# Dilated attention: three PSUM banks for the turns and three for the scores, where it was two and four

## What is computed

```python
proj = (x @ w_in).reshape(B, T, 3, ATT_GROUPS, ATT_HEADS, ATT_HEAD_DIM)   # q, k, v; 3 groups; 16 heads of 64
for g, (window, dil) in enumerate(((128, 1), (512, 4), (2048, 16))):
    s = q @ k.T * hd ** -0.5 + bias[g], masked to a band with step dil
    p_g = softmax(s);  o_g = p_g @ v;  lse_g = log of the denominator
w = softmax over the three groups of lse
return (sum_g w_g * o_g) @ w_out
```

## Time and profile before

| what | us |
|---|---|
| median of 3 runs | 2949.99 |
| lowest and highest | 2945.5, 2952.11 |
| profiled execution, its own time | 2954.55 |
| its span, first to last instruction | 2952.8 |
| PE busy | 2788.1 (94%) |
| DVE busy | 1300.7 (44%) |
| ACT busy | 1017.7 (34%) |
| POOL busy | 191.2 (6%) |

### The profile page before, as it was taken

One profiled execution on the slowest core, in us unless ns is written; L12 is line 12 of the kernel. 1 busy time (PEld: TensorE's weight loads), 2 busy tenths in 40 slices (PEclk: granted clock), 3 DMA queues, 4 the chain that ended last, 5 costly groups with the idle time before them and its releaser, 6 DMA issues.

```text
span 2952.8 us, 40584 instructions
## 1 busy us (share of the span) xinstructions
PE 2788.1 (94%) x17764; PEld 2437.8 (83%) x17764; DVE 1300.7 (44%) x1663; ACT 1017.7 (34%) x1270; POOL 191.2 (6%) x182
## 2 busy tenths in 40 slices
PE   6999999799999999999998979999999989988998
PEld 4778878678787777877887768999989989977997
DVE  3333233264532324333335465556555554554544
ACT  3222232231321223322224244443634444453443
POOL 1000010010100001000001000001010010043100
PEclk9999999967999999999998989999999999999999
DMA  6434354400434335334333214555444545753452
GB/s 241 153 116 164 118 167 136 150 24 1 143 129 137 135 127 173 124 119 157 123 120 133 72 35 152 193 169 172 131 155 161 184 145 191 213 132 108 129 195 77
DMA packets 398176, 406.13 MB, mean 138 GB/s; under 512 B 7216, under 2 KB 397056, under 8 KB 397872
## 3 DMA queue, kind: packets, MB, share of 16 engines
q1 hardware_dynamic: 398000, 403.54, 41.6%
HBM read 402.38 MB, written 1.12 MB: 137 GB/s over the span
## 4 chain that ended last, share of the span: by engine, by line
PE 89%; DVE 5%; ACT 3%; DMA 1%; issue 1%; POOL 0%; SPq 0%; POOLq 0%; ACTq 0%; DVEq 0%
PE bank L96 89%; DVE w_lo L107 1%; ACT w_hi L103 1%; PE bank L99 1%; ACT df_e L104 1%; POOL acc L107 0%; DVE tmp L115 0%; ACT x_hi L103 0%; DMA w_raw<-in_ada_w 0%; SPq L133 0%; DVE x_lo L115 0%; DVE df_e L115 0%; DMA w_raw<-in_even_w_in 0%; DMA w_raw<-in_mix_w_out 0%; DVE df_sc L124 0%
## 5 line engine op out<-in xcount | busy, mean ns | idle before, releaser
L107 DVE TENSOR_TENSOR w_lo<-w_raw,w_hi 128x2048 fp32r<-128x2048 f32 (+2 forms) x331 | 693.8, 2099 | 951.2 <-ACT w_hi L103 950.5
L96 PE MATMUL bank<-x_hi,w_hi 128*128 128x256 f32 (+1 forms) x3128 | 1042.5, 333 | 41.7 <-DVE x_lo L115 25.8
L96 PE MATMUL bank<-x_lo,w_hi 128*128 128x256 f32 (+1 forms) x3128 | 1031.6, 330 | 0.0
L96 PE MATMUL bank<-x_hi,w_lo 128*128 128x256 f32 (+1 forms) x3128 | 1030.9, 330 | 0.0
L103 ACT ACTIVATE w_hi<-w_raw 128x2048 fp32r<-128x2048 f32 (+2 forms) x331 | 578.6, 1751 | 626.1 <-PE bank L96 256.4
L96 PEld LDWEIGHTS bank<-x_hi,w_hi 128*128 128x128 f32 x3128 | 604.7, 193 | 109.9 <-issue 59.8
L96 PEld LDWEIGHTS bank<-x_hi,w_lo 128*128 128x128 f32 x3128 | 604.2, 193 | 51.3
L96 PEld LDWEIGHTS bank<-x_lo,w_hi 128*128 128x128 f32 x3128 | 604.9, 193 | 50.5 <-issue 0.7
L96 PE MATMUL bank<-hid_hi,w_hi 128*128 128x512 f32 (+1 forms) x1056 | 357.2, 338 | 1.3 <-ACT ada_rows L103 1.3
L96 PE MATMUL bank<-hid_hi,w_lo 128*128 128x512 f32 (+1 forms) x1056 | 355.1, 336 | 0.0
L96 PE MATMUL bank<-hid_lo,w_hi 128*128 128x512 f32 (+1 forms) x1056 | 355.1, 336 | 0.0
(11 more groups left out here) (228 smaller groups left out, 2217.5 us busy)
## 6 DMA issues: line engine op xcount, KB each, us to landing
w_raw<-in_ffn_w_in SPq DMA_DIRECT2D x88, 1024.0 KB, 5.9
w_raw<-in_ada_w SPq DMA_DIRECT2D x72, 1024.0 KB, 8.8
w_raw<-in_ffn_w_up SPq DMA_DIRECT2D x44, 1024.0 KB, 5.0
w_raw<-in_attn_w_in SPq DMA_DIRECT2D x36, 1024.0 KB, 4.9
w_raw<-in_ffn_w_out SPq DMA_DIRECT2D x32, 768.0 KB, 5.0
w_raw<-in_ret_w_in SPq DMA_DIRECT2D x24, 1024.0 KB, 5.1
w_raw<-in_ffn_w_out SPq DMA_DIRECT2D x32, 640.0 KB, 4.2
w_raw<-in_odd_w_in SPq DMA_DIRECT2D x12, 1024.0 KB, 5.2
```

Of the source, the lines that this page charges most:

```text
L96: return Issued(self.eng and self.eng.matmul(out, lhsT, rhs, start=start, stop=stop, skip_group_check=loose))
L107: return Issued(self.eng and self.eng.tensor_tensor(out, a, b, op))
```

## The change

The pool of the scores loses bank 3, and the pool of the turns gets it. With three score banks a step's six requests go round the pool twice. `pe_att_scores1` asked for its four banks ahead of its first product; now it asks for each just ahead of the first product that writes it.

```diff
-ATT_SCORES, ATT_TURN, ATT_SUM = (0, 1, 2, 3), (4, 5), (6, 7)
+ATT_SCORES, ATT_TURN, ATT_SUM = (0, 1, 2), (3, 4, 5), (6, 7)
@@ def pe_att_scores1(e, t, p):
-    banks = [[e.bank(("att_s", p, h, i), k.vector, ("att_sum", p, h, i), of=ATT_SCORES) for h in range(2)] for i in range(2)]
     e.wait_ge(k.scalar, ("att", 1, 23))
     for g in range(3):
+        if g != 1:
+            banks = [None, None]
         for h in range(2):
             hs = slice(64 * h, 64 * h + 64)
-            mm = e.matmul(banks[g // 2][h][:, g % 2 * T:(g % 2 + 1) * T], t.q[hs, 8 * g + p, P:T], t.k[hs, 8 * g + p, 0:T],
+            if g != 1:
+                banks[h] = e.bank(("att_s", p, h, g // 2), k.vector, ("att_sum", p, h, g // 2), of=ATT_SCORES)
+            mm = e.matmul(banks[h][:, g % 2 * T:(g % 2 + 1) * T], t.q[hs, 8 * g + p, P:T], t.k[hs, 8 * g + p, 0:T],
                           True, True)
             if g:
                 mm.then_inc(k.product, ("att_s", p, h, g - 1))
```

## The result

| | us |
|---|---|
| changed kernel, median of 4 runs | 2996.16 (2992.43 to 3000.79) |
| kernel before, median of 4 runs | 2947.74 (2943.78 to 2952.11) |
| ratio, 95% interval | 1.0164 (1.0137 to 1.0191) |
| profiled execution after, own time and span | 2995.32, 2993.5 |

48.4 us slower, where 49 were forecast.

What follows compares the result with a forecast made beforehand. PE was taken to bound the kernel, with 89% of the chain that ended last. New waits 35.5 less turn gains 1.4 plus clock 14.8 gave 48.9 us over the median 2949.99: 2999 us, range 2984 to 3012.

Steps and rivals of the forecast that it cites:

- The new wait: Second block's sixth score product on PE waits for DVE's first sum of its own step, eight times, 35.5 us.
- The gain of the third turn bank: Turn waits on PE in the attention that go: 0 in even steps, 0.26 us in odd ones, 1.4 us in all.
- The clock: PE's granted clock falls behind each of the eight new waits, costing 1.85 us each, 14.8 us in all.
- The sum: Whole kernel: new waits less turn gains plus clock loss, 35.5 - 1.4 + 14.8 = 48.9 us slower; chance 0.65.
- the 34.1 put down: PE in the attention: new waits less the turn gains, 35.5 - 1.4 = 34.1 us, without any clock loss.
- The waits without the clock: Rival: in the attention the clock stays at its upper level, only 34.1 us are lost, 2984 us; chance 0.10.
- The clock low throughout: Rival: 10 us behind every new wait run at the low clock, 34 us in all, 3018 us; chance 0.12.
- taken up: Rival: something other than PE holds each piece's end and swallows up to half of each wait, 2972 us; chance 0.08.
- avoided: Rival, not slower: DVE's first sum ends before PE needs its bank, only turn waits count, 2946 us; chance 0.04.

Runs made afterwards that it cites:

- ACT's new order: Kernel before, four score and two turn banks, with ACT's copies of turns 0 and 1 moved ahead of at_hi: median 2935.33 us, ratio 0.9970.
- the filled waits: Three score and two turn banks, extra unread products ahead of the sixth product: ratio 1.0160 with seven, 1.0179 and again 1.0127 with 28.
- With two turn banks: Changed kernel with two turn banks in place of three, still three score banks, bank 3 unused in the attention: ratio 1.0188, attention 201.5 us.
- the second: Changed kernel run once more, unaltered, in a later series of pairs against the kernel before: median 2998.14 us, ratio 1.0184.

## Why the prediction was right, point by point

- **The new wait.** Its place, its releaser and its eight times were as forecast; 34.6 us for 35.5. Odd steps waited 3.93 us for the 4.30 worked out: PE took 1.56 us, not 1.24, to get to the wait, since the end of the fifth product ran alone. Even steps waited 5.71, 5.18 and 5.17 for 5.06, since the third turn bank brought PE there earlier. The two misses cancel in part. From step 3's scores to step 4's it took 20.2 us, for about 20.
- **The gain of the third turn bank.** 1.4 us predicted, 1.6 shown between two and three turn banks. The even steps' turn waits moved to at_lo in full, as said. But the prediction took the turn waits as a matter of banks, and named 14.7 us as all that a third bank could give. They need both, two banks and the copies behind at_hi: a third bank ended them too, for 1.6 us with three score banks, and ACT's new order ended them for 6.3 with four, in which the clock has its part.
- **The clock.** The mechanism was right, and the filled waits show it: 0.42 us for each us at the lower level. Its size was low: 8 x 1.85 = 14.8 us came from 3.4 to 5.0 us at the lower level per wait, some 34 in all. The changed kernel had 58 us there, 51 more than the 6.8 before. Of the 58, 8.5 us lie in PE's idle time and cost nothing; the other 49.5 are 43 more than the 6.6 before, and at 0.42 an estimate of 18 us. What is left of the busy time is near it: 24.4 - 5.5 = 18.9 us. The clock also fell behind the wait of 1.9 us in the middle of the even steps, in two of three steps of the first trace; I had named that wait and not priced it. With two turn banks (waits of 1.61 and 0.25 us there, as before) it fell in two of three too, so the longer single wait isn't shown to be the reason.
- **Left out altogether:** the parting of the fifth and sixth product, 5.5 us by the pieces of the timeline.
- **The sum.** In the attention 31.4 + 5.5 + 18.9 = 55.8 us, for 48.9 forecast. The runs showed 48.4 in the first comparison and 53.2 in the second. (18.9 is what the other two leave, so this sum can't fail to close.) The match with the first comparison is in part luck: two terms were short by 4.1 and 5.5 us, and the net idle time was 2.7 less than the 34.1 put down. Why the runs differ by 2.6 to 7.4 us less than the attentions isn't shown, beyond the 1.6 us that the traces have behind the attention.
- **The rivals.** The waits without the clock, 2984, fell with the clock at 0.85. The clock low throughout fell too: over the 10 us behind each of the eight waits the mean granted clock was 0.66 to 0.83, so it fell behind every one and came back within the step. The wait was not taken up by anything, and not avoided: DVE's sum ended 5.43 us after the scores' start in step 3 and 6.68 in step 4, where it was 6.20, no sooner than before.

Windows of 10 us behind the waits of steps 3, 4 and 6, in the changed kernel:

```profile
2621.97:2631.97 10.00, 10.00 (x73) 8.39 (x74) 2.92 (x5) 1.95 (x4) 1.92 (x2) 0.83 0.33 105
2643.40:2653.40 10.00, 10.00 (x73) 8.27 (x74) 3.02 (x5) 1.95 (x4) 1.92 (x2) 0.83 0.33 105
2691.58:2701.58 10.00, 10.00 (x61) 7.88 (x62) 3.01 (x5) 1.95 (x4) 1.92 (x2) 0.67 0.31 105
```

## What to carry to other kernels

When a bank moves from one pool to another, count the requests of one step against the ring: the first request over its size waits for work of the same step, and what that costs is read from where the freeing instruction stands in its own engine's order. A wait for a buffer need not be cured by a buffer: here a copy stood behind another instruction that was itself waiting, and moving the copy ahead of it made the runs 9.6 us faster (6.3 in the attention) with no bank added. Price a new wait on TensorE with what follows it, its clock and the neighbours that it parts.

## What the runs showed of the hardware that was not expected

Score products of two heads, whose operands stand on rows 0 to 63 and 64 to 127, run side by side: two records, one of each head, take 0.38 us together; the six products take 1.57 us, and 2.38 us when the sixth waits for the fifth. The Trainium skill describes this in "TensorE: Matmul & The Clock Gate", section "Part 3: Packing small matmuls — row/col tiling": small matmuls on different rows of the array overlap. The trace agrees, and adds that a semaphore wait between two of them takes the overlap away.

Seven products of 64 rows in each wait, 3.0 us, left the clock of steps 3 and later as it was (attention at 0.91), and 28 of 128 rows, 3.6 us, kept it up in most steps (0.96). The two differ in rows, in number format and in how long they take, so which of these decides was not separated.
